# Stage edges of a hybrid-attention layer: shifted value rows copied tile by tile by the sync queue, value rows stored later, two tiles read ahead, the last tile in halves

## The reference, cut to what matters

```
u = RMSNorm(h) @ W_in               # split into qa ka va | qb kb vb | xc ac bc | z
o_A: softmax attention over a sliding window of chunks (8 heads, 2 key heads, sinks)
o_B: stick-breaking attention, strictly causal, 128 queries at a time (4 heads)
o_C: gated delta rule after a causal convolution (4 heads)
h <- h + RMSNorm(W_out @ ((o_A | o_B | o_C) * silu(z)))
```

## Time and profile before

| | |
|---|---|
| time, median of 3 runs | 1504.94 us (1501.94 to 1505.55) |
| span of the profiled execution | 1503.7 us |
| own time of the profiled execution | not listed apart; the median of the runs is 1.2 us above the span |
| PE busy | 1418.9 us, 94% |
| DVE, ACT, POOL busy | 790.0, 636.8 and 376.0 us |
| transfers | 177.93 MB, 118 GB/s on average |

### The profile page before, as it was taken

The page is one execution under the profiler, slowest core; times in us unless marked ns, Lnnn a source line. Parts: engine busy times, 40 slices in busy tenths (PEclk is TensorE's granted clock), DMA queues, the critical chain, the costliest instruction groups (busy, mean ns, idle before and its releaser), DMA issues. The chain is left out here.

```text
span 1503.7 us, 32493 instructions
## 1 busy us (share of the span) xinstructions
PE 1418.9 (94%) x13360; PEld 1189.7 (79%) x13360; DVE 790.0 (53%) x1504; ACT 636.8 (42%) x1441; POOL 376.0 (25%) x366
## 2 busy tenths in 40 slices
PE   6999999879999999999999997998998999799996
PEld 5999998868888888888888884664665766687785
DVE  5665666413334333334533325885888886545442
ACT  4454555411112212112211115884665666655551
POOL 0022223222122132222332103550002000055553
PEclk9999999989999999999999998998999999999998
DMA  8644526394443245432145616134100003566651
GB/s 242 183 130 142 157 88 173 110 204 124 130 134 97 70 115 145 129 95 72 51 121 162 178 47 184 61 115 121 44 15 1 15 28 94 159 175 189 202 168 63
DMA packets 203334, 177.93 MB, mean 118 GB/s; under 512 B 30131, under 2 KB 188984, under 8 KB 203192
## 3 DMA queue, kind: packets, MB, share of 16 engines
q1 hardware_dynamic: 154489, 118.42, 27.0%
q0 software_dynamic: 28256, 46.35, 11.0%
q10 hardware_dynamic: 20446, 11.14, 3.0%
HBM read 107.79 MB, written 65.59 MB: 115 GB/s over the span
## 5 line engine op out<-in xcount | busy, mean ns | idle before, releaser
L817 PE MATMUL acc<-side_rows,side_w 128*128 128x384 f32 (+2 forms) x2448 | 458.0, 335 | 15.8 <-ACT side_stage L836 7.8
L817 PEld LDWEIGHTS acc<-side_rows,side_w 128*128 128x128 f32 x2448 | 393.4, 191 | 33.2 <-ACT side_stage L836 7.9
L2047 DVE TENSOR_TENSOR_SCAN prod<-keepb,prod 128x512 f32<-128x512 f32 (+4 forms) x184 | 203.3, 1146 | 52.4 <-ACT keepb L1973 44.5
L709 PE MATMUL acc<-side_rows,side_w 128*128 128x384 f32 (+1 forms) x864 | 149.3, 330 | 0.0
L1282 DVE COPY base<-b_two 128x256 f32<-128x256 f32 x85 | 36.1, 424 | 214.0 <-PE b_two L1071 214.0
L709 PEld LDWEIGHTS acc<-side_rows,side_w 128*128 128x128 f32 x864 | 142.4, 188 | 1.9
L836 ACT ACTIVATE side_stage<-acc 128x384 f32<-128x384 f32 (+2 forms) x102 | 46.8, 461 | 210.9 <-PE acc L817 188.7
L2172 PE MATMUL b_y<-whi,mhi 128*128 128x512 f32 x272 | 108.0, 397 | 8.8 <-DVE wlo L2256 7.6
L1991 ACT ACTIVATE wt<-b_w 128x512 f32<-128x512 f32 (+5 forms) x188 | 88.1, 522 | 58.6 <-PE b_w L1905 58.4
L2172 PE MATMUL b_y<-wlo,mhi 128*128 128x512 f32 x272 | 106.6, 392 | 0.0
L2172 PE MATMUL b_y<-whi,mlo 128*128 128x512 f32 x272 | 106.4, 391 | 0.0
(11 more groups left out here) (249 smaller groups left out, 2314.3 us busy)
## 6 DMA issues: line engine op xcount, KB each, us to landing
side_rows<-hs_scratch POOLq DMA_DIRECT2D x16, 1536.0 KB, 10.3
hs_scratch<-side_rows SPq DMA_DIRECT2D x34, 512.0 KB, 4.7
side_rows<-hs_scratch POOLq DMA_DIRECT2D x6, 1344.0 KB, 10.7
base<-in_x_prompt SPq DMA_DIRECT2D x15, 512.0 KB
mixed<-mix_scratch SPq DMA_DIRECT2D x15, 512.0 KB, 6.7
gates<-sz_scratch SPq DMA_DIRECT2D x15, 512.0 KB, 8.0
xres<-in_x_prompt SPq DMA_DIRECT2D x15, 512.0 KB
out_y_prompt<-yy POOLq DMA_DIRECT2D x15, 512.0 KB, 6.6
```

Source lines behind the costliest of these rows:

```text
L709: last = pe.matmul(acc[:, u % 2, 0:w], side.w[:, c, w_, k, :], h_[:, b % 2, k, 0:w], start=(k == 0 and p == 0), stop=(k == KT - 1 and p == 2))
L817: last = pe.matmul(self.acc[:, n % 2, 0:width], w[:, w_part, k, :], rows[:, row_part, k, 0:width], start=(k == 0 and i == 0), stop=(k == K ...
L2047: dve.tensor_tensor_scan(prod[0:R, hh, c0:c0 + nk][:, ::-1], kv, kv, prod[0:R, hh, c0 + nk:c0 + nk + 1], ALU.mult, ALU.bypass).then_inc(pr ...
```

## The change

Four edits at the edges of stages.

1. The ten stores of value rows leave `rows_and_conv` and are issued by SP in `delta_net`, right behind the store of unit 12. In `rows_and_conv` each weight load of units 32 to 35 is moved ahead of the convolution stores of its unit.
2. The shifted value rows are no longer issued by ACT. SP issues, behind the store of unit 13, the first rows of the tiles as one transfer, and then one transfer a tile (127 partitions, 1 KB in each), two behind each store from unit 13 on, the seventeenth behind that of unit 21. POOL's first subtraction now waits for all 18 of them and for the ten stores.
3. `u_first` holds two tiles, so the first four units of scores read it; the pieces that `window_attention` loads are cut at other tiles.
4. The last tile of `output`: DVE scales and adds each half of the columns, and SP stores each half as two transfers. POOL has no part in it.

```
-    stores = [ (ten pairs of value rows) ]                      # rows_and_conv, SP
+    def value_stores(): return [ (the same ten pairs) ]
...
+    if UNITS - NC + 2 <= q < UNITS:
+        side.load(sp, q - (UNITS - NC))
     if 1 <= b <= NB and i == 3:
         store_conv(b - 1, 4)
         store_conv(b - 1, 5)
...
-    if q == UNITS - 6:
-        sp.wait_ge(row_kept, TILES)
-        for dst, src in stores:
-            sp.dma_start(dst, src).then_inc(out_done, 16)
...
-    if UNITS - NC + 2 <= q < UNITS:
-        side.load(sp, q - (UNITS - NC))
...
     for n in range(first, self.units):                          # transfers: SP in delta_net, first = 8
         self.store(sp, n)
+        early(n - first)
...
+    def value_rows(n):                                          # is early
+        if n == 4:
+            for dst, src in value_stores():
+                sp.dma_start(dst, src).then_inc(values_out, 16)
+        if n == 5:
+            sp.dma_start(vprev[0:1, 1:TILES, :], vrow[P - 1:P, 0:LAST, bcols]).then_inc(prev_in, 16)
+        for m in range(2 * (n - 5), min(2 * (n - 4), TILES)) if n >= 5 else ():
+            sp.dma_start(vprev[1:P, m, :], vrow[0:P - 1, m, bcols]).then_inc(prev_in, 16)
...
-    pool.wait_ge(prev_in, 48)
+    pool.wait_ge(prev_in, 16 * (TILES + 1))
+    pool.wait_ge(values_out, 16 * len(value_stores()))
...
-    def previous_rows():                                        # ACT, at m == 0
-        for to in (slice(1, 113), slice(113, P)):
-            act.dma_start(vprev[to, :, :], vrow[to.start - 1:to.stop - 1, :, bcols]).then_inc(prev_in, 16)
-        act.dma_start(vprev[0:1, 1:TILES, :], vrow[P - 1:P, 0:LAST, bcols]).then_inc(prev_in, 16)
...
-    sp.dma_start(u_first, uT[0:5, :, 0:P]...).then_inc(first_in, 16)
+    sp.dma_start(u_first, uT[0:5, :, 0:2 * P]...).then_inc(first_in, 16)
...
-    PIECES = [1, 2, 4, 8, 12, TILES]
+    PIECES = [1, 3, 4, 8, 12, TILES]
+    STARTS = [2, 3, 4, 8, 12]
...
+    def last_result(s, q):                                      # DVE, output
+        part = slice(0, SP0 + NSAMP)
+        dve.wait_ge(rstd_done, TILES)
+        dve.wait_ge(x_in[s], 32 * q + 32)
+        for c in range(2):
+            cols = slice(c * 512, (c + 1) * 512)
+            dve.scalar_tensor_tensor(out=yy[part, s, cols], in0=b_y[part, s, cols], scalar=rstd[part, s:s + 1], in1=gpost[part, cols],
+                                     op0=ALU.mult, op1=ALU.mult).then_inc(normed, 1)
+            dve.wait_ge(normed, TILES + c)
+            dve.tensor_tensor(yy[part, s, cols], yy[part, s, cols], xres[part, s, cols], ALU.add).then_inc(last_summed, 1)
...
+    for c in range(2):                                          # SP, output, behind all else
+        cols = slice(c * 512, (c + 1) * 512)
+        sp.wait_ge(last_summed, c + 1)
+        sp.dma_start(yp[SEQ - SP0:SEQ, cols], yy[0:SP0, s, cols]).then_inc(last_out, 16)
+        sp.dma_start(io["y_sample"][0][:, cols], yy[SP0:SP0 + NSAMP, s, cols]).then_inc(last_out, 16)
```

More of the change, by code:

```diff
@@ L141, in wide, with value_stores @@
             return a.to_broadcast(shape)
+        def value_stores():
+            rows = lambda name: io[name][0, 0].rearrange("t h d -> t (h d)")
+            b0 = slice(VAW, VAW + VBW)
+            return [(rows("p_b_v")[0:NMETA, :], vrow[PAD:CH, 0, b0]),
+                      (rows("p_b_v")[NMETA:NMETA + CH, :], vrow[CH:P, 0, b0]),
+                      (rows("p_b_v")[NMETA + CH:NMETA + SEQ - SP0, :].rearrange("(t p) n -> p t n", p=P), vrow[:, 1:LAST, b0]),
+                      (rows("p_b_v")[NMETA + SEQ - SP0:NMETA + SEQ, :], vrow[0:SP0, LAST, b0]),
+                      (rows("s_b_v"), vrow[SP0:SP0 + NSAMP, LAST, b0]),
+                      (rows("p_a_v")[0:WIN - SP0, :], vrow[SP0:P, LAST - 1, 0:VAW]),
+                      (rows("p_a_v")[WIN - SP0:WIN, :], vrow[0:SP0, LAST, 0:VAW]),
+                      (rows("s_a_v")[WIN - NSAMP:WIN, :], vrow[SP0:SP0 + NSAMP, LAST, 0:VAW]),
+                      (rows("s_a_v")[0:WIN - NSAMP, :], rows("cache_a_v")[NSAMP:WIN, :]),
+                      (rows("s_a_k")[0:WIN - NSAMP, :], rows("cache_a_k")[NSAMP:WIN, :])]
         def rows_and_conv(cx, acc, side, begun):
@@ L360, in _ @@
                         sp.wait_ge(zero_out, 64)
-                        sp.wait_ge(out_done, 16 * (len(stores) + 2))
+                        sp.wait_ge(out_done, 32)
                         sp.wait_ge(s0_in, 32)
@@ L864, in store, with transfers @@
                 sp.dma_start(self.tiles[t][1][:, c0:c0 + width], self.stage[:, n % 2, 0:width]).then_inc(self.stored[n % 2], 16)
-            def transfers(self, sp, first, beside):
+            def transfers(self, sp, first, early, beside):
                 for t in range(2):
@@ L958, in first_rows @@
                                 sp.wait_ge(side.stored[i], 16 * NB * side.first_size // 2)
-                            sp.dma_start(u_first, uT[0:5, :, 0:P].rearrange("k p t -> p k t")).then_inc(first_in, 16)
+                            sp.dma_start(u_first, uT[0:5, :, 0:2 * P].rearrange("k p t -> p k t")).then_inc(first_in, 16)
                             sp.dma_start(sink, io["sinks_a"].to_broadcast([P, AH])).then_inc(first_in, 16)
-                        side.transfers(sp, begun, first_rows)
+                        def value_rows(n):
[6 more added lines that the diff above has]
+                                sp.dma_start(vprev[1:P, m, :], vrow[0:P - 1, m, bcols]).then_inc(prev_in, 16)
+                        side.transfers(sp, begun, value_rows, first_rows)
                         sp.wait_ge(first_in, 32)
@@ L1465, in load_piece @@
                         def load_piece(i):
-                            rows = slice(PIECES[i] * P if i else 0, PIECES[i + 1] * P)
+                            rows = slice(PIECES[i] * P, PIECES[i + 1] * P)
                             sp.dma_start(reg[:, 0:5, rows], uT[0:5, :, rows].rearrange("k p t -> p k t")).then_inc(u_in[i], 16)
@@ L1496, in scores @@
                                 pe.wait_ge(exp_done, AG * (n - 1))
-                            if s == 0 and m in PIECES[:-1]:
-                                pe.wait_ge(u_in[PIECES.index(m)], 16)
+                            if s == 0 and m in STARTS:
+                                pe.wait_ge(u_in[STARTS.index(m)], 16)
                             half = [slice(j * CH, (j + 1) * CH) for j in range(AKV)]
@@ L1515, in scores @@
                             for j, u in slots:
-                                rows = u_first if m == 0 else reg
+                                rows = u_first if m < 2 else reg
                                 qh, at = rows[half[j], 2 * s + u, q0:q0 + R], 2 * j + u
@@ L2089, in output @@
                 mix_in, x_in, y_out = ([sem(f"{n}{i}", st) for i in range(3)] for n in ("mix_in", "x_in", "y_out"))
-                names = "gpost_in w_hi w_lo z_sig z_gated gated m_hi m_lo y_ready sq_done ln_done rstd_done normed summed".split()
+                names = "gpost_in w_hi w_lo z_sig z_gated gated m_hi m_lo y_ready sq_done ln_done rstd_done normed summed last_summed last_out".split()
                 (gpost_in, w_hi, w_lo, z_sig, z_gated, gated, m_hi, m_lo, y_ready, sq_done, ln_done, rstd_done, normed,
-                 summed) = (sem(n, st) for n in names)
+                 summed, last_summed, last_out) = (sem(n, st) for n in names)
                 xp, yp = io["x_prompt"][0], io["y_prompt"][0]
@@ L2240, in low @@
                                               ALU.subtract).then_inc(m_lo, 1)
+                        def last_result(s, q):
[8 more added lines that the diff above has]
+                                dve.tensor_tensor(yy[part, s, cols], yy[part, s, cols], xres[part, s, cols], ALU.add).then_inc(last_summed, 1)
                         def norm(n, s, q):
+                            if exact(n) and n == LAST:
+                                last_result(s, q)
+                                return
                             dve.wait_ge(rstd_done, n + 1)
@@ L2268, in result @@
                         def result(n, s, q):
-                            part = slice(CH, P) if exact(n) and n == 0 else slice(0, SP0 + NSAMP if exact(n) and n == LAST else P)
+                            if exact(n) and n == LAST:
+                                return
+                            part = slice(CH, P) if exact(n) and n == 0 else slice(0, P)
                             if exact(n) and n == 0:
@@ L2290, in _ @@
                         for s in range(3):
-                            pool.wait_ge(y_out[s], 32 * len([n for n in range(TILES) if n % 3 == s]))
+                            pool.wait_ge(y_out[s], 32 * len([n for n in range(LAST) if n % 3 == s]))
         def stage(work, *args, **kwargs):
```

25 lines of the change are left out of this document (5 added, 20 removed).

## The result

The changed kernel takes 1540.28 us (median of 4 runs, 1539.85 to 1543.28) against 1503.6 us before (median of 4, 1501.94 to 1505.55): ratio 1.0244, 95% interval 1.0227 to 1.0262. That is 36.7 us slower, where 81 were forecast. The profiled execution took 1539.85 us with a span of 1538.2.

A forecast was written before the change was run, and what follows sets the result against it. PE, busy 94% of the span, was taken to bound the kernel. Edits: -3.4 - 9.5 + 96.5 + 0 - 2.5 = +81.1 on the 1503.7 us span, 1584.8, plus 1.2 for the median: 1586 us, range 1488 to 1632.

The forecast's parts named there:

- the price of one copy: delta_net: a 127-partition tile copy runs on one DMA engine and takes 9.0 us, bounds 7.5 and 9.7; seventeen take 153 us.
- The lower bound: One tile copy in delta_net takes at least 7.5 us, from 158 rows out of HBM at 59 ns each.
- the prediction's own sum: delta_net: copies from 355.6, plus 153, sharing and a 2.1 us landing; unit 26 starts near 522.2, PE stands 96.5 us.
- the lost clock: delta_net: PE's clock loss within the 96.5 us of standing is hidden under the copies, so nothing was added.
- Rival (b): delta_net: one engine at 27 GB/s, 4.8 us a copy, PE stands 15 us; about 1504, 1515 with sharing; chance 0.08.
- Its turning point: The whole change turns from faster to slower at some 4.9 us a copy.
- Rival (a): delta_net: copies spread over the engines, 0.6 us a tile, hidden; gains stand alone, 1489.5 us; chance 0.19.
- Rival (c): delta_net: stores land past the copies, but POOL waits for all copies, 520 against 480, 40 us; 1529 us; chance 0.05.
- second price: POOL's first subtraction moves with its tile by 96 us, to about 577; copies have landed by then, so no extra cost.
- Sharing: The copying engine's sixteenths of other work in delta_net: 7 us for a pair of row loads, 4 for nine side stores.
- Where PE stands: delta_net: PE waits 96.5 us behind ACT's keep of side units, some 10 us per unit over units 17 to 26.
- Edit 2, what it removes: First tile of delta_net: PE's 7.6 us wait for ACT's keep goes, and 1.9 us of low clock; -9.5, bounds -7.6 and -9.7.

The follow-up runs named there:

- the split version: The changed kernel with each 127-partition tile copy on SP cut into two of 112 and 15 partitions: 1490.18 us, ratio 0.99 to the kernel before.
- the splits: The changed kernel with each tile copy cut into 112 and 15 partitions (1490.18 us), or into 126 and 1 (1487.89 us).
- the stores on ACT: The changed kernel with side stores issued by ACT behind its keep, copies staying on SP: units 13 to 24, 1532.07 us; units 13 to 40, 1507.09 us.
- runs with the old copies: Chiefly the changed kernel with the three shifted-row copies back on ACT at the first tile, edits 1, 3 and 4 kept: 1497.44 us, ratio 0.9953.

## Why the prediction was right in sign and wrong in size

**The step that failed** is the price of one copy: "This is the same data and the same kind of transfer, so I take a value near it, 9.0." It came from sixteen engines copying together, 13.4 GB/s each. One engine alone moves 22.3 GB/s and takes 5.82 us. The lower bound failed as well: 7.5 us came from rows out of HBM, 59 ns each, and inside on-chip memory a row takes 46 ns. Seventeen copies at 5.82 are 98.9 us instead of 153. Put into the prediction's own sum that gives 355.6 + 98.9 + 11 + 2.1 + 0.5 = 468.1 for the start of unit 26 and 42.4 us of PE standing behind 425.7, where 96.5 were forecast; all edits together then give +27.0 for a measured +36.7. Measured against the split version the cost is 51.4, and the windows over delta_net in the changed and in the split kernel show what it consists of:

```profile
300.50:948.50 648.00, 599.08 (x6931) 532.29 (x6931) 218.83 (x657) 122.23 (x327) 145.25 (x200) 0.96 0.41 113
```

```profile
301.50:898.10 596.60, 587.35 (x6931) 522.39 (x6932) 218.65 (x657) 123.09 (x327) 145.26 (x200) 1.00 0.44 123
```

PE is idle 48.9 us and 9.3, 39.7 more, and takes 11.7 us more for the same products, at a clock of 0.96 for 1.00. Two smaller terms were low: the row loads took 10.5 us for 7, and the first tile copy was issued 13.4 us behind the keep of unit 12 (332.94 to 346.38) where 10.5 were forecast. With them the sum gives 48.9. The trace agrees: counted from delta_net's first product, ACT keeps unit 22 at 143.6 us (444.06) and in the split version at 95.0 (396.48), 48.6 later, and PE's last long wait ends there:

```profile
444.06 0.49 ACT L835 ACTIVATE side_stage<-acc 128x384 f32<-128x384 f32 x1 [9.19 <-DMA uT_scratch<-side_stage]
...
444.88 0.70 PE L1093 MATMUL b_two<-base 64*64 64x64 f32 x16 [8.00 <-ACT base L1198]
```

The prediction called the lost clock hidden under the copies. Within these 48.6 us it is, by this sum, but not behind the last wait: from 443.9 to 450 PE was busy 5.1 us at a clock of 0.50, which costs 2.6. Together that is 51.2 of the 51.4. The chain itself is shown by the splits and by the stores on ACT.

The Trainium skill's page "DMA: Bandwidth & Descriptors" (section "Why a DMA increments its semaphore by 16 and not by 1") gives 127 partitions one engine, and the runs agree for copies inside on-chip memory too: 126 partitions, which 14 divides, cost what 112 and 15 cost. The section "Specifications" of that page of the Trainium skill gives an engine ~27 GiB/s, which no copy here reached: 22.3 GB/s alone, 13.4 in company.

**Rival (b)**, one engine as fast as its tail, had the right idea of an engine alone, and its 4.8 us a copy is nearer to 5.82 than the 7.5 of my bound (1.0 below, 1.7 above). Its turning point, 4.9 us a copy, agrees with the sign: at 5.82 the kernel is slower. **Rival (a)** was false here but names what the split gives, 1489.5 forecast and 1490.2 measured. **Rival (c)** was false: the stores stood in line. POOL's first subtraction moved from 480.3 to 519.7, with its tile; no second price, as forecast.

**Sharing** was taken as 11 us, 7 for the row loads and 4 for the side stores. The one pair beside row loads paid 10.5, and nine stores at 0.42 are 3.8.

**Where PE stands**: forecast for ACT's keep alone. It is longer in the wait for `base` (23.5 us in 7 waits), since ACT works in order and its delta-rule copies queue behind a keep that waits.

**Edit 2, what it removes**: -9.5 forecast. The copies off ACT's queue give 10.3 us in delta_net against runs with the old copies and 12.4 against the profile of before.

**Edit 1**: -3.4 forecast, 2.0 to 3.9 by the stage. The weight load does go out earlier. **Edit 3**: 0 forecast, 0 measured, and the reason holds: the cached values' place in the queue was the limit, and once it was moved the read-ahead was worth 3.9 us of the stage. **Edit 4**: -2.5 forecast, 2.9 by the ratio, 3.8 by the tail; the last store of SP lands at 1535.31 + 1.9 = 1537.2, 1.0 us ahead of the span's end, where POOL's of before landed 2.6 us ahead of it (1501.1 and 1503.7), a gap that the forecast had left as it was.

## What to carry to other kernels

Before a copy is cut by tile, look at its partition count: 127 cost 5.8 us and held everything behind it in the queue, 126 + 1 or 112 + 15 cost next to nothing. A price for one DMA engine isn't to be taken as a sixteenth of a full transfer's rate: look for a stretch in which one engine works alone, over the same memories. And when a wait moves to another name without the time moving, as `reg` to `vc` here, the limit is the order of the queue: change that order, and the edit that seemed worthless may pay.

## What was not expected of the hardware

- An engine alone copies 1 KB rows inside on-chip memory at 22.3 GB/s; with all sixteen at work each moved 13.4.
- While that engine has a copy under way, SP is held at its next issues (5.7 us for a side store that takes 0.33 otherwise), so whatever SP would do later, also a transfer of another kind, is late too.
- The landing of the same 64 KB behind the same 1.2 MB varied between 6.2 and 9.8 us from issue among eleven profiled runs, enough to look like an effect of an edit.
- The end of rows_and_conv takes one of two lengths with the same code, 65.3 to 65.4 us (five profiles) or 66.8 to 67.0 (five). What differs is the clock of the 24 products behind a wait of PE for ACT's keep near 280 us: 1.00 and 2.9 us in the shorter ones, 0.55 and 4.5 us in the longer ones. That wait was 1.9 us in all the longer ones and 0.3 in four of the shorter; in the fifth, side stores 13 to 40 on ACT's queue, it was 1.95 us too and the clock stayed. What decides it was not looked for with a run.
